# Second attention of a two-block kernel: the sink becomes a 257th logit column, fillers are split in halves, output chunk 0 is finished first

## The chip, the cores and the metric

The kernel runs on one core of one Trainium2 chip. The metric is the device time of one execution in microseconds (us), lower is better. Three runs of the kernel before gave 1569.63, 1569.12 and 1566.43 us (median 1569.12). Traces are taken in an execution of their own.

## What is computed

Two transformer blocks over 512 tokens of width 1024 in fp32. The first block has two layers: a gated linear recurrence with a convolutional feed-forward part, and then a sliding-window attention with a sink, again with a feed-forward part. The second block mixes pooling, a forgetting attention and a memory attention. The change lies in the sliding-window attention, which has 16 query heads of width 64, 4 key/value heads and a window of 128 over 128-token blocks:

```python
logits = einsum(q, kk) * scale + bias            # 128 queries x 256 keys (block j-1 and j)
logits = where(mask, logits, -inf)
m = maximum(logits.max(-1), sink)                # sink: one learned number per query head
p = exp(logits - m[..., None])
denom = p.sum(-1) + exp(sink - m)
o = einsum(p, vv) / denom
return o.reshape(B, S, D) @ w_out
```

## The kernel before

Everything is written by hand, engine by engine, in program order, with semaphores between the engines. Each large matrix product is done in three fp32r matmuls (high*high, low*high, high*low parts), so activations and weights are kept as a high and a low half: `AH`/`AL`, `OH`/`OL`, `WH`/`WL`. Weights come in 1 MB chunks, in one order, through two slots: SyncE loads `RAW`, ScalarE writes the high half (`split_hi`, `split_next`, L1155), GpSimd writes the low half in four instructions (`split_cols` L444, `split_rows` L453), TensorE uses the chunk and releases its slot (`w_used`). `EXTRAS` are a few chunks with slots of their own, whose low half VectorE writes (`extra_low`, L1767).

The second attention (calls `sw_...`) works in 16 units, `SW_UNITS`: a unit is one pair of heads b (two heads, x) with two query blocks (t), so four rows of 256 logits. For unit i:

- TensorE `sw_score(i)` (L868) makes the scores in `bank[0]`. It waits for the logits of unit i-1, and for every fourth unit for the next query chunk `QB`.
- VectorE `sw_logits(i)`: scale and bias into `PL` (L2001), maximum of the row (L2004), minimum with the negated sink (L2006), sink minus maximum (L2008), which releases the unit (`l_ready`).
- ScalarE `sw_expo(i)`: the exponential of the sink (L1447), then of the four rows with their sums (L1450).
- VectorE `sw_weights(i)`: sum plus sink (L2013), reciprocal (L2015), four row scalings (L2018), which release `p_ready`.
- TensorE `sw_turn(i)` (L881), eight transposes of `PL`; ScalarE copies them to `PT` (L1472); TensorE `sw_weigh(i)` (L895) multiplies by the values `VT`; for every second unit VectorE `sw_finish` writes `OH`/`OL` (L2025, L2027).

The order of the engines: VectorE does logits(i+1), perhaps finish, weights(i). ScalarE does expo(i+1), the copy of unit i, and after units 1, 5 and 9 `sw_query`: it copies the next query chunk (L1456) and splits one more weight chunk (L1155), whose low half GpSimd then makes. TensorE does, for u from 0 to 15, score(u+2), turn(u), weigh(u-1), and fills with independent work, called fillers here: quarters of the query chunks 1 to 3 (`sw_piece`, 12 matmuls of 512 columns) for u up to 9, and pieces of the first two output chunks N_SO and N_SO+1 (`sw_mixed(j, ms)`, output blocks `ms` of chunk j, 6 matmuls each) from u=10. What is left of these follows the last unit, and then `last_rows` uses N_SO+2 and N_SO+3, which are split only when the slots of N_SO and N_SO+1 are released.

Of the kernel before, what the change touches and what calls it, by code (L numbers as in the profile page):

```python
# [29 lines left out]
P = 128  # L30
# [59 lines left out]
def build(nc, stream, x_t, mem_t, params, consts, masks, sinks, rel_in, w_pool, out):  # L90
# [6 lines left out]
    with ExitStack() as ctx:  # L97
# [25 lines left out]
        SMALL = sb("SMALL", [P, 4, 3, 4])  # L123
# [5 lines left out]
        INV = sb("INV", [P, 2, T])  # L129
        par = {k: PAR[:, a:b] for k, (a, b) in PCOL.items()}  # L130
# [3 lines left out]
        NMAX, SUMS, SNK, RDEN = (SMALL[:, i] for i in range(4))  # L134
# [12 lines left out]
        with ExitStack() as s:  # L147
# [11 lines left out]
            with ExitStack() as s1:  # L159
                BIAS = sb("BIAS", [P, SWH, 2 * P], F32, s1)  # L160
                KT = sb("KT", [P, 2, T], F32, s1)
                VT = sb("VT", [P, TT, 2 * P], F32, s1)
                QB = sb("QB", [P, 8, T], F32, s1)
                PL = sb("PL", [P, 3, 4, 2 * P], F32, s1)
                PT = sb("PT", [P, 2, 8, P], F32, s1)
# [67 lines left out]
        def bk(i):  # L233
            return bank[i // 2][:, i % 2]
# [41 lines left out]
        sg_made, pool_w_loaded = sem("sg_made"), sem("pool_w_loaded")  # L276
# [200 lines left out]
        def _(pe):  # L477
# [362 lines left out]

            def sw_piece(c, piece):

                if piece == 0 and c == 1:
                    pe.wait_ge(v_copied_sw, 1)
                if piece == 0 and c > 1:
                    pe.wait_ge(qb_copied, c)
                n = SQ_CHUNK[c]
                col_chunk(n, slot(n), (bk(6), bk(7)), AH, AL, ks=(2 * piece, 2 * piece + 1))
# [59 lines left out]
            for u in range(16):  # L908
                if u + 2 < 16:
                    sw_score(u + 2)  # L910
                if u == 0:
                    pe.wait_ge(qb_copied, 1)
                sw_turn(u)
                if u == 0:
                    sw_piece(1, 1)
                    sw_piece(1, 2)
                if u == 1:
                    sw_piece(1, 3)
                    pe.wait_ge(v_copied_sw, 1)
                if u == 5:  # L920
                    sw_piece(2, 3)
                if u == 9:
                    sw_piece(3, 3)
                if u == 15:
                    pe.wait_ge(l_ready, 16)
                    sw_mixed(0, (2, 3))
                if u:
                    sw_weigh(u - 1)
                if 2 <= u < 5:
                    sw_piece(2, u - 2)  # L930
                if 6 <= u < 9:
                    sw_piece(3, u - 6)
                if u == 10:
                    pe.wait_ge(qb_copied, 4)
                    pe.wait_ge(o_ready, 10)
                    sw_mixed(0, (0,))
                if u == 11:
                    sw_mixed(0, (1,))
                if u == 12:
                    pe.wait_ge(o_ready, 12)  # L940
                    sw_mixed(1, (0,))
                if u == 13:
                    sw_mixed(1, (1,))
            sw_weigh(15)
            pe.wait_ge(pt_ready, 16)
            sw_mixed(0, (4, 5))
            sw_mixed(1, (2, 3))
            pe.wait_ge(o_ready, 16)
            sw_mixed(0, (6, 7))
            sw_mixed(1, (4, 5, 6, 7))  # L950
# [197 lines left out]
        def _(act):  # L1148
# [312 lines left out]
            sw_query(0)  # L1461
            sw_expo(0)
# [3 lines left out]
            for i in range(16):  # L1466
# [118 lines left out]
        def _(dve):  # L1585
# [397 lines left out]
            SINK3 = SINK[:, :].rearrange("p (o x b) -> p o x b", o=2, x=2)  # L1983
            BIAS5 = BIAS[:, :, :].rearrange("p (o x b) s -> p o x b s", o=2, x=2)

            def sw_logits(i):
# [3 lines left out]
                nmax, snk = (a[:, s].rearrange("p (x t) -> p x t", t=2) for a in (NMAX, SNK))  # L1990
                bias = BIAS5[:, b // 4, :, b % 4]
                sink = SINK3[:, b // 4, :, b % 4].unsqueeze(2).broadcast_to([P, 2, 2])
# [6 lines left out]
                for t in range(2):  # L1999
                    lo = P if tiles[t] == 0 else 0  # L2000
                    dve.scalar_tensor_tensor(rows[:, :, t, lo:], bank[0][:, :, 256 * t + lo:256 * t + 256], SCALE, bias[:, :, lo:],  # L2001
                                             ALU.mult, ALU.add)
                dve.drain()
                dve.tensor_reduce(nmax, rows, AX_X, ALU.max, negate=True)  # L2004
                dve.drain()
                dve.scalar_tensor_tensor(nmax, sink, -1.0, nmax, ALU.mult, ALU.min)  # L2006
                dve.drain()
                dve.tensor_tensor(snk, sink, nmax, ALU.add).then_inc(l_ready, 1)  # L2008

            def sw_weights(i):  # L2010
                s = i % 3
                dve.wait_ge(p_exp, i + 1)
                dve.tensor_tensor(SUMS[:, s], SUMS[:, s], SNK[:, s], ALU.add)  # L2013
                dve.drain()
                dve.reciprocal(RDEN[:, s], SUMS[:, s])  # L2015
                dve.drain()
                for r in range(4):
                    ins = dve.tensor_scalar(PL[:, s, r], PL[:, s, r], RDEN[:, s, r:r + 1], None, ALU.mult)  # L2018
# [316 lines left out]
```

## Time and profile before

| | |
|---|---|
| median of three runs | 1569.12 us (1566.43 to 1569.63) |
| the profiled execution | 1567.07 us, span 1565.3 us |
| TensorE busy (PE) | 1497.5 us, 96% |
| VectorE busy (DVE) | 900.5 us, 58% |
| ScalarE busy (ACT) | 611.4 us, 39% |
| GpSimd busy (POOL) | 510.7 us, 33% |
| mean granted TensorE clock | 0.992 |

The time is that of the whole program; the span runs from its first to its last recorded instruction. PE is the matmul row of the profile, DVE, ACT and POOL the rows of VectorE, ScalarE and GpSimd. The second attention's units lie between 737 and 855 us of the span, and the end of its output product between 855 and 887 us.

### The profile page before, as it was taken

To read this page: it belongs to the slowest core of one execution; us is meant where nothing else is said; L and a number is where in the kernel's file an instruction comes from. 1 tells how busy PE (TensorE), PEld (TensorE's weight loads), DVE (VectorE), ACT (ScalarE), POOL (GpSimd) and SP (SyncE) were. 2 spreads that over 40 slices of the span, in tenths; PEclk is the share of its full clock that TensorE was granted. 3 is DMA by queue.
4 is the path that set the end of the run, shared out by engine and by line. 5 is a ranking of instruction groups with operands and counts; after the bars stand their busy time and mean duration, and the time that the engine had idled before them with its cause. 6 is when DMAs were issued, how large, how long until landed. Compare 5 with 4: busy or idle time off the path is not lost.

```text
span 1565.3 us, 21457 instructions
## 1 busy us (share of the span) xinstructions
PE 1497.5 (96%) x8174; PEld 1254.0 (80%) x8174; DVE 900.5 (58%) x1315; ACT 611.4 (39%) x768; POOL 510.7 (33%) x380
## 2 busy tenths in 40 slices
PE   7999999999999999999997999999999989999889
PEld 5888888798888888889775888888888887777667
DVE  7778686576566550145686576556620283655741
ACT  3554455344322231235564442332221254555520
POOL 3000002215454554532210335545444533323212
PEclk9999999999999999999999999999999999999999
DMA  8511111412322223332202112232222222312201
GB/s 226 131 55 55 69 67 54 148 68 81 108 82 106 88 99 108 107 108 82 81 28 81 54 53 89 102 107 80 107 88 100 103 98 83 108 58 74 88 27 54
DMA packets 22583, 137.22 MB, mean 88 GB/s; under 512 B 2488, under 2 KB 4840, under 8 KB 7280
## 3 DMA queue, kind: packets, MB, share of 16 engines
q1 hardware_dynamic: 17280, 124.79, 22.5%
q10 hardware_dynamic: 5232, 11.45, 3.0%
q8 instruction: 48, 0.79, 0.2%
q14 instruction: 23, 0.19, 0.0%
HBM read 132.02 MB, written 4.21 MB: 87 GB/s over the span
## 4 chain that ended last, share of the span: by engine, by line
issue 58%; POOL 25%; PE 14%; ACT 1%; DVE 1%; ACTq 0%; DMA 0%; DVEq 0%; POOLq 0%; SPq 0%
POOL WL L444 16%; POOL WL L453 9%; PE pair L480 4%; PE pair L481 3%; PE pair L482 3%; PE pair L1048 1%; PE pair L1035 1%; ACT WH L1155 1%; PE pair L967 1%; ACTq L1486 0%; DVE PL L2146 0%; DMA RAW<-stream 0%; PE pair L1025 0%; ACT PL L1490 0%; ACT L1509 0%
## 5 line engine op out<-in xcount | busy, mean ns | idle before, releaser
L444 POOL TENSOR_TENSOR WL<-RAW,WH 128x512 fp32r<-128x512 f32 x240 | 327.5, 1397 | 490.7 <-ACT WH L1155 490.7
L480 PE MATMUL pair<-AH,WH 128*128 128x512 f32 (+1 forms) x1240 | 472.6, 381 | 14.3 <-POOL WL L444 11.4
L481 PE MATMUL pair<-AL,WH 128*128 128x512 f32 (+1 forms) x1240 | 463.0, 373 | 0.0
L482 PE MATMUL pair<-AH,WL 128*128 128x512 f32 (+1 forms) x1240 | 462.7, 373 | 0.0
L1155 ACT ACTIVATE WH<-RAW 128x2048 fp32r<-128x2048 f32 x108 | 206.6, 1914 | 474.9 <-PE pair L482 460.4
L453 POOL TENSOR_TENSOR WL<-RAW,WH 128x512 fp32r<-128x512 f32 x136 | 183.0, 1377 | 545.2 <-ACT WH L1155 545.2
L480 PEld LDWEIGHTS pair<-AH,WH 128*128 128x128 f32 x1240 | 233.6, 188 | 60.1 <-POOL WL L444 11.4
L482 PEld LDWEIGHTS pair<-AH,WL 128*128 128x128 f32 x1240 | 233.4, 188 | 41.8
L481 PEld LDWEIGHTS pair<-AL,WH 128*128 128x128 f32 x1240 | 233.7, 188 | 40.5 <-issue 1.9
L1940 DVE TENSOR_SCALAR CA<-pair,PAR 128x512 f32<-128x512 f32 x88 | 67.3, 806 | 148.2 <-PE pair L482 145.2
L480 PE MATMUL pair<-GH,WH 128*128 (+2 forms) x416 | 150.4, 361 | 0.0
L482 PE MATMUL pair<-GH,WL 128*128 (+2 forms) x416 | 149.9, 360 | 0.0
L481 PE MATMUL pair<-GL,WH 128*128 (+2 forms) x416 | 149.9, 360 | 0.0
L1945 DVE SCALAR_TENSOR_TENSOR CA<-pair,PAR,CA 128x510 f32<-128x510 f32 (+1 forms) x176 | 123.8, 745 | 14.4 <-issue 13.8
L480 PE MATMUL pair<-OH,WH 128*128 128x512 f32 (+1 forms) x256 | 90.3, 353 | 2.4 <-POOL WL L453 2.4
L480 PEld LDWEIGHTS pair<-GH,WH 128*128 128x128 f32 x416 | 78.2, 188 | 13.5 <-POOL WL L453 0.2
L481 PEld LDWEIGHTS pair<-GL,WH 128*128 128x128 f32 x416 | 78.2, 188 | 13.3
L482 PEld LDWEIGHTS pair<-GH,WL 128*128 128x128 f32 x416 | 78.2, 188 | 13.0
L481 PE MATMUL pair<-OL,WH 128*128 128x512 f32 (+1 forms) x256 | 87.6, 342 | 0.0
L482 PE MATMUL pair<-OH,WL 128*128 128x512 f32 (+1 forms) x256 | 87.4, 341 | 0.0
L1767 DVE TENSOR_TENSOR WL<-RAW,WH 128x1024 fp32r<-128x1024 f32 x14 | 20.1, 1481 | 103.6 <-ACT WH L1169 103.5
L480 PE MATMUL pair<-WH,AH 128*128 128x256 f32 (+1 forms) x192 | 59.9, 312 | 3.8 <-DVE AL L1851 2.9
(245 smaller groups left out, 2012.9 us busy)
## 6 DMA issues: line engine op xcount, KB each, us to landing
RAW<-stream SPq DMA_DIRECT2D x115, 1024.0 KB, 4.8
H<-x_t SPq DMA_DIRECT2D x3, 1024.0 KB, 8.9
bias_rows<-ROWS ACTq DMA_DIRECT2D x1, 2048.0 KB, 24.9
BIAS<-bias_rows ACTq DMA_DIRECT2D x1, 2048.0 KB, 7.7
FBC<-forget_rows ACTq DMA_DIRECT2D x4, 512.0 KB, 4.0
out<-H ACTq DMA_DIRECT2D x8, 256.0 KB, 2.0
H<-x_t SPq DMA_DIRECT2D x2, 512.0 KB, 6.1
CON<-consts ACTq DMA_DIRECT2D x1, 513.5 KB, 4.3
```

The costliest lines, as they stand in the source:

```text
L444: pool.tensor_tensor(WL[w][:, part], RAW[raw][:, part], WH[w][:, part].bitcast(F32), ALU.subtract).then_inc(w_lo, 1)
L453: pool.tensor_tensor(wl[:, :, part], raw[:, :, part], wh[:, :, part].bitcast(F32), ALU.subtract).then_inc(w_lo, 1)
L480: pe.matmul(out_, wh, xh, start=start, stop=False, skip_group_check=shared)
L481: pe.matmul(out_, wh, xl, start=False, stop=False, skip_group_check=shared)
L482: return pe.matmul(out_, wl, xh, start=False, stop=stop, skip_group_check=shared)
L967: pe.matmul(bk(5), con["mean64"], SQH[:, :], start=True, stop=True).then_inc(n_summed, 1)
L1035: mm = pe.transpose(bk(2 + x)[:, at:at + P], PL2[:, i % 3, x, at:at + P], con["ident"])
L1048: mm = pe.matmul(bk(4)[64 * x:64 * x + 64, n * P:n * P + P], (VM if kind == "mem" else VF)[:, kb, c0:c0 + 64], PT2[:, i % 2, x, 256 * t + ...
L1155: act.activation(WH[w][:, :], RAW[raw][:, :], ACT.Copy).then_inc(w_hi, 1)
L1767: dve.tensor_tensor(WL[w][:, part], RAW[w][:, part], WH[w][:, part].bitcast(F32), ALU.subtract).then_inc(e_lo, 1)
L1940: dve.tensor_scalar(out_[:, c], src[:, c], tap[2], CONVB[:, layer, ab, blk], ALU.mult, ALU.add)
L1945: ins = dve.scalar_tensor_tensor(out_[:, c, d:T], src[:, c, 0:T - d], CONVW[:, layer, 2 - d, ab, blk], out_[:, c, d:T], ALU.mult, ALU.add)
```

## The change

1. `PL` rows are 264 wide instead of 256. ScalarE copies the sink of the head into column 256 (`sw_sink`): three times ahead of unit 0, and after the copy of unit i for unit i+3. The maximum runs over 257 columns and the exponentials with their sums too. L2006, L2008 and L2013 on VectorE and L1447 on ScalarE are gone, and `SMALL` loses a row. The maximum waits for the sink's copy (`sink_put`).
2. The fillers of TensorE: for u=1, 5, 9 the quarter of a query chunk stands ahead of turn(u) instead of behind it; for u=3, 4, 7, 8 half of it (`sw_half`, 6 matmuls) stands ahead of turn(u) and half behind weigh(u-1); the output pieces of u=10 to 13 stand at u=11 to 14, ahead of turn(u), and that of u=15 too.
3. Behind the last unit, output blocks 6 and 7 of chunk 0 come ahead of blocks 2 and 3 of chunk 1.

```diff
-        SMALL = sb("SMALL", [P, 4, 3, 4])
+        SMALL = sb("SMALL", [P, 3, 3, 4])
...
-                PL = sb("PL", [P, 3, 4, 2 * P], F32, s1)
+                PL = sb("PL", [P, 3, 4, 2 * P + 8], F32, s1)
...
+            def sw_half(c, piece, m):
+                if (piece, m) == (0, 0):
+                    pe.wait_ge(qb_copied, c)
+                n = SQ_CHUNK[c]
+                wh, wl = wcols(slot(n))
+                for k in (2 * piece, 2 * piece + 1):
+                    if m == 0 and k % 2 == 0:
+                        lo_ready(n, k // 2)
+                    mm = three(bk(6 + m), wh[:, k, m * P:m * P + P], wl[:, k, m * P:m * P + P], AH[:, k], AL[:, k], k == 0, k == KB - 1)
+                if (piece, m) == (3, 1):
+                    mm.then_inc(w_used, 1)
...
+                if u == 1:
+                    sw_piece(1, 3)
+                if u in (3, 4, 7, 8):
+                    sw_half(2 + u // 6, (u - 1) % 4 - 1, 0)
+                if u in (5, 9):
+                    sw_half(2 + u // 6, 3, 0)
+                    sw_half(2 + u // 6, 3, 1)
+                if u == 11:
+                    sw_mixed(0, (0,))
+                if u == 12:
+                    sw_mixed(0, (1,))
+                if u == 13:
+                    pe.wait_ge(o_ready, 12)
+                    sw_mixed(1, (0,))
+                if u == 14:
+                    sw_mixed(1, (1,))
+                if u == 15:
+                    pe.wait_ge(l_ready, 16)
+                    sw_mixed(0, (2, 3))
                 sw_turn(u)
                 if u == 0:
                     sw_piece(1, 1)
                     sw_piece(1, 2)
                 if u == 1:
-                    sw_piece(1, 3)
                     pe.wait_ge(v_copied_sw, 1)
-                if u == 5:
-                    sw_piece(2, 3)
-                if u == 9:
-                    sw_piece(3, 3)
-                if u == 15:
-                    pe.wait_ge(l_ready, 16)
-                    sw_mixed(0, (2, 3))
                 if u:
                     sw_weigh(u - 1)
-                if 2 <= u < 5:
-                    sw_piece(2, u - 2)
-                if 6 <= u < 9:
-                    sw_piece(3, u - 6)
+                if u in (2, 6):
+                    sw_half(2 + u // 6, 0, 0)
+                    sw_half(2 + u // 6, 0, 1)
+                if u in (3, 4, 7, 8):
+                    sw_half(2 + u // 6, (u - 1) % 4 - 1, 1)
                 if u == 10:
                     pe.wait_ge(qb_copied, 4)
                     pe.wait_ge(o_ready, 10)
-                    sw_mixed(0, (0,))
-                if u == 11:
-                    sw_mixed(0, (1,))
-                if u == 12:
-                    pe.wait_ge(o_ready, 12)
-                    sw_mixed(1, (0,))
-                if u == 13:
-                    sw_mixed(1, (1,))
+            pe.wait_ge(pt_ready, 16)
             sw_weigh(15)
-            pe.wait_ge(pt_ready, 16)
             sw_mixed(0, (4, 5))
-            sw_mixed(1, (2, 3))
             pe.wait_ge(o_ready, 16)
             sw_mixed(0, (6, 7))
-            sw_mixed(1, (4, 5, 6, 7))
+            sw_mixed(1, (2, 3, 4, 5, 6, 7))
             last_rows(2, 3, OH, OL)
...
-                act.activation(SNK[:, s], SNK[:, s], ACT.Exp)
                 for r in range(4):
-                    row = PL[:, s, r]
+                    row = PL[:, s, r, 0:2 * P + 1]
...
+            def sw_sink(i):
+                _, b, _ = SW_UNITS[i]
+                act.activation(PL[:, i % 3, :, 2 * P].rearrange("p (x t) -> p x t", t=2),
+                               SINK3[:, b // 4, :, b % 4].unsqueeze(2).broadcast_to([P, 2, 2]), ACT.Copy).then_inc(sink_put, 1)
...
+            for i in range(3):
+                sw_sink(i)
             sw_expo(0)
...
                 act.activation(PT[:, i % 2].rearrange("p (x k) c -> p x (k c)", x=2), bank[1][:, :, :], ACT.Copy).then_inc(pt_ready, 1)
+                if i + 3 < 16:
+                    sw_sink(i + 3)
...
-                dve.tensor_reduce(nmax, rows, AX_X, ALU.max, negate=True)
-                dve.drain()
-                dve.scalar_tensor_tensor(nmax, sink, -1.0, nmax, ALU.mult, ALU.min)
-                dve.drain()
-                dve.tensor_tensor(snk, sink, nmax, ALU.add).then_inc(l_ready, 1)
+                dve.wait_ge(sink_put, i + 1)
+                dve.tensor_reduce(nmax, rows[:, :, :, 0:2 * P + 1], AX_X, ALU.max, negate=True).then_inc(l_ready, 1)
...
-                dve.tensor_tensor(SUMS[:, s], SUMS[:, s], SNK[:, s], ALU.add)
-                dve.drain()
```

On VectorE, the logits and weights of one unit. Before (from logits(9) to the start of logits(10)):

```order
L2001 SCALAR_TENSOR_TENSOR PL<-pair,BIAS 128x2x256 x2
L2004 TENSOR_REDUCE SMALL<-PL 128x4
L2006 SCALAR_TENSOR_TENSOR SMALL<-SINK,SMALL 128x4
L2008 TENSOR_TENSOR SMALL<-SINK,SMALL 128x4
L2013 TENSOR_TENSOR SMALL<-SMALL 128x4
L2015 RECIPROCAL SMALL<-SMALL 128x4
L2018 TENSOR_SCALAR PL<-PL,SMALL 128x256 x4
L1997 MEMSET PL 128x2x128
```

The same place now:

```order
L2021 SCALAR_TENSOR_TENSOR PL<-pair,BIAS 128x2x256 x2
L2025 TENSOR_REDUCE SMALL<-PL 128x4
L2030 RECIPROCAL SMALL<-SMALL 128x4
L2033 TENSOR_SCALAR PL<-PL,SMALL 128x256 x4
L2017 MEMSET PL 128x2x128
```

Three small instructions of a unit are gone; the rest keeps its order.

On TensorE, u=11: score(13), turn(11), weigh(10) and a piece of the output product (`OH`, `OL` with `WH`, `WL`). Before:

```order
L868 MATMUL pair<-KT,QB 128x256 x4
L881 MATMUL pair<-CON,PL 128x128 x8
L895 MATMUL pair<-PT,VT 64x128 x6
L480 MATMUL pair<-OH,WH 128x512
L481 MATMUL pair<-OL,WH 128x512
L482 MATMUL pair<-OH,WL 128x512
```

Now:

```order
L879 MATMUL pair<-KT,QB 128x256 x4
L481 MATMUL pair<-OH,WH 128x512
L482 MATMUL pair<-OL,WH 128x512
L483 MATMUL pair<-OH,WL 128x512
L481 MATMUL pair<-OH,WH 128x512
L482 MATMUL pair<-OL,WH 128x512
L483 MATMUL pair<-OH,WL 128x512
L892 MATMUL pair<-CON,PL 128x128 x8
L906 MATMUL pair<-PT,VT 64x128 x6
```

The six matmuls that stood behind weigh now stand between the scores and the transposes.

On ScalarE, what follows expo(6): the copy of unit 5, the query chunk, the split. Before:

```order
L1472 ACTIVATE PT<-pair 128x1024
L1456 ACTIVATE QB<-pair 128x1024
L1155 ACTIVATE WH<-RAW 128x2048
L1447 ACTIVATE SMALL<-SMALL 128x4
L1450 ACTIVATE PL,SMALL<-PL,SMALL 128x256 x4
```

Now:

```order
L1492 ACTIVATE PT<-pair 128x1024
L1468 ACTIVATE PL<-SINK 128x4
L1474 ACTIVATE QB<-pair 128x1024
L1169 ACTIVATE WH<-RAW 128x2048
L1463 ACTIVATE PL,SMALL<-PL,SMALL 128x257 x4
```

The small instruction ahead of the exponentials is gone, and one of the same size stands behind the copy of the transposes, ahead of the query copy. (Lines shift by the added code.)

## Rows read from the trace of the kernel before

**Rows 1.** Waits of TensorE, 753 to 890 us: total, times, longest.
```profile
PE pair L881 <- DVE PL L2018: 10.9, 6, 3.1
PE pair L480 <- POOL WL L453: 2.1, 1, 2.1
PE pair L868 <- DVE SMALL L2008: 1.0, 1, 1.0
```

**Rows 2.** Timeline of TensorE, units 2 to 6: start, duration, instructions, [idle before].
```profile
766.21 0.93 PE L868 MATMUL pair<-KT,QB 64*128 64x128 f32 x8 [0.27 <-ACT QB L1456]
...
768.09 1.15 PE L895 MATMUL pair<-PT,VT 128*64 128x128 f32 x16
...
772.10 1.14 PE L868 MATMUL pair<-KT,QB 64*128 64x256 f32 x8
774.96 1.09 PE L881 MATMUL pair<-CON,PL 128*128 128x128 f32 x8 [1.72 <-DVE PL L2018]
...
791.77 0.49 PE L868 MATMUL pair<-KT,QB 64*128 64x128 f32 x4 [0.27 <-ACT QB L1456]
```

**Rows 3.** Timeline of TensorE, the last units.
```profile
832.94 1.15 PE L895 MATMUL pair<-PT,VT 128*64 128x128 f32 x16
835.61 1.14 PE L868 MATMUL pair<-KT,QB 64*128 64x256 f32 x8
...
847.99 1.97 PE L881 MATMUL pair<-CON,PL 128*128 128x128 f32 x8 [3.09 <-DVE PL L2018]
853.34 1.80 PE L895 MATMUL pair<-PT,VT 128*64 128x128 f32 x28
```

**Rows 4.** Timeline of VectorE: logits(11), weights(10), then logits(12).
```profile
813.90 1.22 DVE L2004 TENSOR_REDUCE SMALL<-PL 128x4 f32<-128x1024 f32 x1
815.20 0.16 DVE L2006 SCALAR_TENSOR_TENSOR SMALL<-SINK,SMALL 128x4 f32<-128x4 f32 x1
815.43 0.16 DVE L2008 TENSOR_TENSOR SMALL<-SINK,SMALL 128x4 f32<-128x4 f32 x1
815.51 0.16 DVE L2013 TENSOR_TENSOR SMALL<-SMALL 128x4 f32<-128x4 f32 x1
815.74 0.18 DVE L2015 RECIPROCAL SMALL<-SMALL 128x4 f32<-128x4 f32 x1
816.00 1.14 DVE L2018 TENSOR_SCALAR PL<-PL,SMALL 128x256 f32<-128x256 f32 x4
...
819.38 1.22 DVE L2004 TENSOR_REDUCE SMALL<-PL 128x4 f32<-128x1024 f32 x1
820.67 1.00 DVE L2006 SCALAR_TENSOR_TENSOR SMALL<-SINK,SMALL 128x4 f32<-128x4 f32 x1
821.75 1.15 DVE L2008 TENSOR_TENSOR SMALL<-SINK,SMALL 128x4 f32<-128x4 f32 x1
```

**Rows 5.** Timeline of ScalarE and of GpSimd at the query chunk of unit 9.
```profile
816.23 1.03 ACT L1456 ACTIVATE QB<-pair 128x1024 f32<-128x1024 f32 x1 [1.72 <-PE pair L482]
817.15 1.90 ACT L1155 ACTIVATE WH<-RAW 128x2048 fp32r<-128x2048 f32 x1
...
819.13 4.98 POOL L453 TENSOR_TENSOR WL<-RAW,WH 128x512 fp32r<-128x512 f32 x4 [20.52 <-ACT WH L1155]
```

**Rows 6.** Timeline of VectorE and of GpSimd in the memory attention, from 1372 us.
```profile
1375.04 3.01 DVE L2146 TENSOR_SCALAR PL<-PL,SMALL 128x256 f32<-128x256 f32 x4 [0.44 <-issue]
...
1372.31 5.07 POOL L444 TENSOR_TENSOR WL<-RAW,WH 128x512 fp32r<-128x512 f32 x4 [12.81 <-ACT WH L1155]
```

**Rows 7.** Windows: length, busy and count of PE, PEld, DVE, ACT, POOL, then PEclk.
```profile
827.40:830.60 3.20, 3.20 (x15) 2.48 (x13) 2.47 (x9) 2.16 (x7) 0.00 (x0) 0.50 0.30 125
847.90:851.10 3.20, 3.12 (x12) 2.83 (x13) 0.03 (x1) 1.11 (x2) 0.00 (x0) 0.50 0.00 0
```

**Rows 8.** Timeline of GpSimd and ScalarE at the end of the output product.
```profile
865.76 11.97 POOL L453 TENSOR_TENSOR WL<-RAW,WH 128x512 fp32r<-128x512 f32 x8 [41.65 <-ACT WH L1155]
...
869.37 1.92 ACT L1155 ACTIVATE WH<-RAW 128x2048 fp32r<-128x2048 f32 x1 [1.88 <-PE pair L482]
```

More of the change, by code:

```diff
@@ L129, in build @@
         INV = sb("INV", [P, 2, T])
+        SINK3 = SINK[:, :].rearrange("p (o x b) -> p o x b", o=2, x=2)
         par = {k: PAR[:, a:b] for k, (a, b) in PCOL.items()}
@@ L133, in build @@
         CONVB = par["conv_b"].rearrange("p (l a j) -> p l a j", l=2, a=2)
-        NMAX, SUMS, SNK, RDEN = (SMALL[:, i] for i in range(4))
+        NMAX, SUMS, RDEN = (SMALL[:, i] for i in range(3))
         with ExitStack() as s:
@@ L275, in build @@
         fox_v_mm, fox_v, vm_copied, half_mm, o_taken = (sem(n) for n in ("fox_v_mm", "fox_v", "vm_copied", "half_mm", "o_taken"))
-        sg_made, pool_w_loaded = sem("sg_made"), sem("pool_w_loaded")
+        sg_made, pool_w_loaded, sink_put = sem("sg_made"), sem("pool_w_loaded"), sem("sink_put")
         z_abs, z_exp, f_made, f_stored = (sem(n) for n in ("z_abs", "z_exp", "f_made", "f_stored"))
@@ L844, in sw_piece @@
                     pe.wait_ge(v_copied_sw, 1)
-                if piece == 0 and c > 1:
-                    pe.wait_ge(qb_copied, c)
                 n = SQ_CHUNK[c]
@@ L1981, in _ @@
             layer_norm(1)
-            SINK3 = SINK[:, :].rearrange("p (o x b) -> p o x b", o=2, x=2)
             BIAS5 = BIAS[:, :, :].rearrange("p (o x b) s -> p o x b s", o=2, x=2)
@@ L1989, in sw_logits @@
                 rows = PL[:, s].rearrange("p (x t) s -> p x t s", t=2)
-                nmax, snk = (a[:, s].rearrange("p (x t) -> p x t", t=2) for a in (NMAX, SNK))
+                nmax = NMAX[:, s].rearrange("p (x t) -> p x t", t=2)
                 bias = BIAS5[:, b // 4, :, b % 4]
-                sink = SINK3[:, b // 4, :, b % 4].unsqueeze(2).broadcast_to([P, 2, 2])
                 dve.drain()
@@ L2000, in sw_logits @@
                     lo = P if tiles[t] == 0 else 0
-                    dve.scalar_tensor_tensor(rows[:, :, t, lo:], bank[0][:, :, 256 * t + lo:256 * t + 256], SCALE, bias[:, :, lo:],
+                    dve.scalar_tensor_tensor(rows[:, :, t, lo:2 * P], bank[0][:, :, 256 * t + lo:256 * t + 256], SCALE, bias[:, :, lo:],
                                              ALU.mult, ALU.add)
                 dve.drain()
-                dve.tensor_reduce(nmax, rows, AX_X, ALU.max, negate=True)
-                dve.drain()
-                dve.scalar_tensor_tensor(nmax, sink, -1.0, nmax, ALU.mult, ALU.min)
-                dve.drain()
-                dve.tensor_tensor(snk, sink, nmax, ALU.add).then_inc(l_ready, 1)
+                dve.wait_ge(sink_put, i + 1)
+                dve.tensor_reduce(nmax, rows[:, :, :, 0:2 * P + 1], AX_X, ALU.max, negate=True).then_inc(l_ready, 1)
             def sw_weights(i):
@@ L2017, in sw_weights @@
                 for r in range(4):
-                    ins = dve.tensor_scalar(PL[:, s, r], PL[:, s, r], RDEN[:, s, r:r + 1], None, ALU.mult)
+                    ins = dve.tensor_scalar(PL[:, s, r, 0:2 * P], PL[:, s, r, 0:2 * P], RDEN[:, s, r:r + 1], None, ALU.mult)
                 ins.then_inc(p_ready, 1)
```

## The prediction, made before the changed kernel ran

> **What bounds the kernel now.** I read the waits of TensorE first, because TensorE is busy for 96% of the span and is the only engine whose idle time can be won. In and behind the second attention it waits 10.9 us in six places for the row scalings of VectorE, 1.0 us for VectorE's logits, and 2.1 us for a low half of GpSimd at the output product [rows 1]. Then I read the timelines of the engines. TensorE shows two regimes. With 12-matmul fillers four units take 25.56 us (766.21 to 791.77) and TensorE idles only 0.27 + 1.72 of them [rows 2]: it is the bound. In the last five units the fillers are 6 matmuls, and it waits at nearly every turn, 3.09 us at the last one [rows 3]: there VectorE is the bound, whose logits, finish and weights stand in one line. Last I read the granted clock: it falls to 0.50, which is 1.2 GHz, for 3.2 us each at 827.4 and 847.9, both times just behind idle stretches of TensorE [rows 7].
>
> **How I cost it.** The change alters orders on three engines that release each other, so I carried it forward step by step: each step starts when its engine is free and its last releaser is done, plus the 0.05 us or so that rows show between engines, with durations from the rows. On the order of before this gives scores(8) at 791.69 and scores(12) at 817.16 (trace: 791.77 [rows 2], and 817.31, just behind the query copy that ends at 817.26 [rows 5]) and the last transposes at 847.07 (847.99 [rows 3]; the clock fall at 827 is the difference). So it may be trusted to some tenths of a us. With the new order it gives the terms below.
>
> **VectorE's unit.** From the end of the maximum (813.90 + 1.22 = 815.12) to the logits' release (815.59) two small instructions cost 0.47 us; L2013 delays the reciprocal by 0.23 more [rows 4]. The memory attention of this kernel has exactly the new sequence, and there the reciprocal follows the maximum at once. So weights end 0.70 us earlier in each unit. One more column in the maximum and in an exponential costs about a nanosecond a row: nothing. The small exponential's 0.11 us in front of ScalarE's rows goes too, and the sink's copy, of the same size, stands behind the copy of the transposes. The new wait for it costs nothing: that copy is issued three units ahead, about 5 us before the maximum needs it. The scalings still read 256 columns in one run, so I leave their 1.14 us for four [rows 4]; were the wider row pitch to make them slower, only five units are on the path. The bounds of the 0.70 are 0.47 (nothing won at L2013) and 0.70.
>
> The Trainium skill, page "VectorE: DVE Perf Modes", section on the TRN2 errata, gives 58 + N cycles for an SBUF source, an estimate of 0.065 us for each of the three. By that the unit would win 0.2 us and not 0.70, and the stage some 2.5 us less. The rows decide, since they show the gaps too.
>
> **GpSimd beside VectorE.** At unit 12 the two removed instructions took 1.00 and 1.15 us in place of 0.16 [rows 4], while GpSimd's four splits ran from 819.13 to 824.11 [rows 5]; the same at units 4 and 8. That is 1.84 us gone each time. But the scalings then come 2.5 us earlier, into the same GpSimd stretch, and the memory attention shows what four scalings cost there: 3.01 us instead of 1.14, each waiting for the end of one GpSimd instruction [rows 6]. In the steps this makes weights(3), (7) and (11) end 1.55 us later than alone. For units 3 and 7 that is hidden behind the half filler with 0.8 us to spare; for unit 11 it is not.
>
> This is a rule of the Trainium skill that speaks against the change: page "SBUF — State Buffer", section "Who interferes with whom", says that a scaling in the two-port mode and a GpSimd instruction exclude each other for the whole instruction. The trace agrees, with the 3.01 us. By the rule each scaling issued under GpSimd waits separately, which is the sum here; without it the forecast would be 1.5 us better.
>
> **Units 0 to 11 (query fillers).** Splitting a filler costs: 12 matmuls take 772.10 - 768.09 - 1.07 = 2.94 us [rows 2], six take 835.61 - 832.94 - 1.08 = 1.59 [rows 3]. Four splits cost 4 x 0.26 = 1.0 us. At u=1, 5, 9 the filler now stands ahead of the transposes, so scores(4), (8), (12) come right behind weigh, while the query copy comes behind the copy of the transposes: 1.09 transposes + 1.02 copy + 0.12 sink + 1.03 query copy, against 1.02 + 0.86 or 1.08 of TensorE work. It waits 1.40 us where it waited 0.27 [rows 2, 5], three times: +3.4. What goes are the 1.72 us waits at turn(3) and turn(7) [rows 2]: -3.4. So scores(12) start at 818.42 instead of 817.31: **+1.1 us**. The first eleven units win nothing.
>
> **Units 11 to 15 (VectorE bound).** From scores(12) to the last transposes before takes 847.99 - 817.31 = 30.7 us. Here four logits save 0.47 and five weights 0.23 (-3.0), the GpSimd collisions change by -1.84 + 1.55, and the clock fall at 827 with its 0.75 us on the path is absent; against that some scores come 0.5 us later, behind a filler and a turn. The steps give 845.51 - 818.42 = 27.1: **-3.6 us**.
>
> **Behind the last transposes.** Before, 847.99 to 855.07 (the end of the weighing) is 7.1 us, with a 12-matmul filler of 2.94 in it and the clock at half for 3.2 us, which costs 1.56 [rows 3, 7]. Now that filler lies ahead of the transposes, in the 3.09 us of waiting. Left are transposes, the two weighings and a 0.33 wait for the last copy, 3.3 us: **-3.8 us**.
>
> **Output product.** 20 pieces of work stay. Chunk 0 is used up 12 matmuls earlier, 2.8 to 2.9 us. That releases ScalarE's split and GpSimd's four instructions for N_SO+2 by as much, and the wait of 2.1 us [rows 1] goes. N_SO+3 becomes next: its slot is released at 869.37 as before, its fourth low part would be there at 869.37 + 1.92 + 5.0 = 876.4, and TensorE asks for it at 876.45 [rows 8]. That is just hidden, bounds 0 to 0.5: **-2.1 us**.
>
> **Sum.** 1.1 - 3.6 - 3.8 - 2.1 = -8.4 us. It counts on no clock fall. One like that at 827 costs 0.75 to 1.6; between 821 and 829 the new order still idles 0.4 + 1.8 + 0.9 us, where the old one idled 3.0 and fell. I take off 0.4 for it: **-8.0 us**. The profiled execution took 1567.07 us, so its like would take 1559.1; it lies 2.05 below the median of the three runs, 1569.12, and on the median the forecast is 1561.1 us. Everything behind the stage moves as a block, since its loads are released by the progress of the engines.
>
> **Rivals.**
> - *Half of it* (chance 0.20): the collisions are worse than 1.55 in units 3 and 7, where only 0.8 us of cover is left, and the clock falls as often as before. Both falls back cost 2.3, two more collisions up to 1.5 each beyond the cover, giving 2.5 to 5 us, 1564 to 1566.5. For it speaks that idle stretches of 1.4 us come in at three new places; against it that the 1.72 us idle of before brought no fall.
> - *No change that can be told* (0.08): the change does not do what it says, because the row scalings move wholly under GpSimd at each query chunk and scores wait for the query copy by more than 1.4 us, say 3 us when the split stands ahead. That makes units 0 to 11 lose 5 us more. Then 1566 to 1571.
> - *More* (0.08): VectorE's shorter unit lets TensorE close nearly all of the 14.0 us of waits [rows 1] and the slow clock. The 1.40 waits stand against it: 10 to 12 us, 1557 to 1559.
> - *Slower* (0.05): the clock. From 818 to 829 TensorE idles in four short pieces. If it were granted half speed there and did not come back until the end of the units at 849, 31 us at half would cost up to 15 us, 1566 to 1576. It ends above before if half speed lasts over 16 us. The two falls of before lasted 3.2 us each and ended in dense work [rows 7], which comes back at 849 at the latest.
> - The forecast, 5 to 10 us won, has 0.59.
>
> **How the numbers follow.** About 0.2% (3.1 us) is what a measurement of this kernel can tell from no change. Faster by more: the forecast, the rival with more, and most of the half (0.15): 0.82. Within: the rest of the half and the third case: 0.13. Slower: 0.05. The range goes from 1557, which takes in the case with more, to 1566, which takes in most of the half; outside are about two in ten.
>
> **What would show it.** The waits of TensorE for the scalings should fall from 10.9 to under 3 us, with turn(3), turn(7) and the last turn gone; scores(4), (8), (12) should wait about 1.4 us each for the query copy; four scalings of weights(3), (7), (11) should take 2.5 to 3 us; the 2.1 us wait at N_SO+2 should be gone, with none or a short one at N_SO+3; the clock windows should show at most one fall. The prediction is wrong if a new wait stands on `sink_put`, if the clock falls at scores(4) or (8), or if the stretch ahead of scores(12) grows by more than 2 us.

## The result and the profile after

The changed kernel takes 1557.14 us (median of 4 runs, 1556.08 to 1557.67) beside 1567.84 for the kernel before (4 runs, 1566.43 to 1569.63). The ratio is 0.9921, 95% interval 0.9907 to 0.9934, which is 10 to 15 us; the medians themselves differ by 10.7 us, a ratio of 0.9932, and the two profiled executions by 9.8 (1567.07 and 1557.29). The forecast of 8.0 us had the sign and the mechanisms, and was too small.

The page's heading and its busy times (busy us, share, instructions) for the kernel after:

```profile
span 1555.5 us, 21361 instructions
PE 1494.0 (96%) x8174; PEld 1250.0 (80%) x8174; DVE 889.1 (57%) x1267; ACT 610.7 (39%) x768; POOL 510.5 (33%) x380
```

VectorE has 48 instructions less, three for each unit, and 11.4 us less work. TensorE runs the same number of matmuls, but it is not only its idle time that went. Over the stage (from a mark at its start to the layer norm behind it, both defined in the next section) its row reads, first before and then after (length, busy and count of PE, PEld, DVE, ACT, POOL, then PEclk):

```profile
749.86:888.46 138.60, 122.62 (x837) 96.73 (x837) 92.64 (x202) 68.90 (x167) 32.02 (x24) 0.98 0.17 62
750.39:879.00 128.61, 119.63 (x836) 94.46 (x836) 83.48 (x157) 68.39 (x165) 32.24 (x24) 1.00 0.19 66
```

So 7.0 of the 10.0 us were idle time, and 3.0 us were busy time: the same matmuls, some of them at the lower clock in the kernel before. The waits of TensorE after, 753 to 890 us (total, times, longest), to be read against [rows 1]:

```profile
PE pair L879 <- ACT QB L1474: 3.8, 3, 1.3
PE pair L892 <- DVE PL L2033: 2.1, 3, 1.4
PE pair L583 <- DVE H L1810: 1.5, 1, 1.5
PE pair L879 <- DVE SMALL L2025: 1.2, 2, 0.8
PE pair L906 <- ACT PT L1492: 0.3, 1, 0.3
```

The waits for the row scalings fell from 10.9 to 2.1 us, that for GpSimd at the output product is gone, and three waits of 1.3 us for the query copy are new in size: they were 0.27 us each. The timeline of TensorE after shows the four units of [rows 2], and then the end of [rows 3]. The matmuls of the fillers (L481 to L483) between these rows are left out:

```profile
767.79 0.93 PE L879 MATMUL pair<-KT,QB 64*128 64x128 f32 x8 [1.26 <-ACT QB L1474]
768.65 1.09 PE L892 MATMUL pair<-CON,PL 128*128 128x128 f32 x8
769.67 1.15 PE L906 MATMUL pair<-PT,VT 128*64 128x128 f32 x16
773.69 1.13 PE L879 MATMUL pair<-KT,QB 64*128 64x256 f32 x8
776.25 1.04 PE L892 MATMUL pair<-CON,PL 128*128 128x128 f32 x8
777.22 0.93 PE L906 MATMUL pair<-PT,VT 128*64 128x128 f32 x12
779.68 0.93 PE L879 MATMUL pair<-KT,QB 64*128 64x128 f32 x8
...
785.65 1.14 PE L879 MATMUL pair<-KT,QB 64*128 64x256 f32 x8
789.58 1.04 PE L892 MATMUL pair<-CON,PL 128*128 128x128 f32 x8
790.55 0.93 PE L906 MATMUL pair<-PT,VT 128*64 128x128 f32 x12
792.74 0.93 PE L879 MATMUL pair<-KT,QB 64*128 64x128 f32 x8 [1.26 <-ACT QB L1474]
...
844.39 1.09 PE L892 MATMUL pair<-CON,PL 128*128 128x128 f32 x8
845.41 0.93 PE L906 MATMUL pair<-PT,VT 128*64 128x128 f32 x12
846.68 1.12 PE L906 MATMUL pair<-PT,VT 128*64 128x128 f32 x16 [0.35 <-ACT PT L1492]
```

From the first marked scores to the second, four units take 24.95 us where they took 25.56. Within them TensorE waits once, the 1.26 us at their start. turn(3) at 776.25 does not wait although its scalings run into GpSimd until 775.35 (their row is the first below), since the half filler stands in front of it. At the end the last transposes wait for nothing, where they waited 3.09 us. The timelines of VectorE and of GpSimd after, at units 11 and 12 (the counterpart of [rows 4, 5]):

```profile
772.79 2.56 DVE L2033 TENSOR_SCALAR PL<-PL,SMALL 128x256 f32<-128x256 f32 x4
...
819.72 1.22 DVE L2025 TENSOR_REDUCE SMALL<-PL 128x4 f32<-128x1028 f32 x1
821.03 0.69 DVE L2040 CAST OH<-pair 128x512 fp32r<-128x512 f32 x1
821.80 0.69 DVE L2042 TENSOR_TENSOR OL<-pair,OH 128x512 fp32r<-128x512 f32 x1
822.41 0.17 DVE L2030 RECIPROCAL SMALL<-SMALL 128x4 f32<-128x4 f32 x1
822.65 2.53 DVE L2033 TENSOR_SCALAR PL<-PL,SMALL 128x256 f32<-128x256 f32 x4
825.35 1.29 DVE L2021 SCALAR_TENSOR_TENSOR PL<-pair,BIAS 128x512 f32<-128x512 f32 x2 [0.16 <-issue]
826.71 1.22 DVE L2025 TENSOR_REDUCE SMALL<-PL 128x4 f32<-128x1028 f32 x1
827.85 0.17 DVE L2030 RECIPROCAL SMALL<-SMALL 128x4 f32<-128x4 f32 x1
828.10 1.14 DVE L2033 TENSOR_SCALAR PL<-PL,SMALL 128x256 f32<-128x256 f32 x4
```

```profile
819.47 5.04 POOL L454 TENSOR_TENSOR WL<-RAW,WH 128x512 fp32r<-128x512 f32 x4 [19.85 <-ACT WH L1169]
```

The maximum over 1028 elements still takes 1.22 us, and the four scalings of unit 11 take 2.53 us while GpSimd works and 1.14 us in unit 12, when it does not. The granted clock after, in windows, shows no fall where [rows 7] showed two:

```profile
820.00:836.00 16.00, 13.16 (x104) 9.62 (x101) 14.24 (x28) 11.05 (x37) 4.51 (x4) 1.00 0.19 66
836.00:852.00 16.00, 15.14 (x112) 11.78 (x111) 9.42 (x19) 6.96 (x12) 0.00 (x0) 1.00 0.38 132
```

### The profile page after: what moved, and what is told of

Read it like the earlier page. It is cut to its first block, busy times and chain, and to the rows that moved or that the text cites. A ratio compares the mean times of both kernels' runs of the same rounds, so it can differ in the third digit from the quotient of the medians.

```text
span 1555.5 us, 21361 instructions
## 1 busy us (share of the span) xinstructions
PE 1494.0 (96%) x8174; PEld 1250.0 (80%) x8174; DVE 889.1 (57%) x1267; ACT 610.7 (39%) x768; POOL 510.5 (33%) x380
## 4 chain that ended last, share of the span: by engine, by line
issue 58%; POOL 25%; PE 14%; ACT 1%; DVE 1%; ACTq 0%; DMA 0%; DVEq 0%; POOLq 0%; SPq 0%
POOL WL L445 16%; POOL WL L454 9%; PE pair L481 4%; PE pair L482 3%; PE pair L483 3%; PE pair L1062 1%; PE pair L1049 1%; ACT WH L1169 1%; PE pair L981 1%; ACTq L1508 0%; DVE PL L2161 0%; DMA RAW<-stream 0%; PE pair L1039 0%; ACT PL L1512 0%; ACT L1531 0%
## 5 line engine op out<-in xcount | busy, mean ns | idle before, releaser
L481 PE MATMUL pair<-AH,WH 128*128 128x512 f32 (+1 forms) x1240 | 473.6, 382 | 14.6 <-POOL WL L445 11.5
L483 PE MATMUL pair<-AH,WL 128*128 128x512 f32 (+1 forms) x1240 | 462.9, 373 | 0.0
L481 PEld LDWEIGHTS pair<-AH,WH 128*128 128x128 f32 x1240 | 233.6, 188 | 62.1 <-POOL WL L445 11.8
L483 PEld LDWEIGHTS pair<-AH,WL 128*128 128x128 f32 x1240 | 233.4, 188 | 42.2
L481 PE MATMUL pair<-GH,WH 128*128 (+2 forms) x416 | 149.6, 360 | 0.1
L483 PE MATMUL pair<-GH,WL 128*128 (+2 forms) x416 | 149.0, 358 | 0.0
L481 PE MATMUL pair<-OH,WH 128*128 128x512 f32 (+1 forms) x256 | 89.2, 349 | 0.4 <-POOL WL L454 0.4
L481 PEld LDWEIGHTS pair<-GH,WH 128*128 128x128 f32 x416 | 78.0, 188 | 14.0 <-POOL WL L454 0.5
L483 PEld LDWEIGHTS pair<-GH,WL 128*128 128x128 f32 x416 | 77.9, 187 | 13.3
L483 PE MATMUL pair<-OH,WL 128*128 128x512 f32 (+1 forms) x256 | 86.6, 338 | 0.0
L1251 ACT ACTIVATE DD<-DD 128x1024 f32<-128x1024 f32 x28 | 29.5, 1055 | 86.7 <-DVE DD L1672 86.7
```

The source lines that it names most:

```text
L481: pe.matmul(out_, wh, xh, start=start, stop=False, skip_group_check=shared)
L483: return pe.matmul(out_, wl, xh, start=False, stop=stop, skip_group_check=shared)
L1251: act.activation(DD[:, lv % 2], DD[:, lv % 2], ACT.Exp).then_inc(level_exp, 1)
```

## The stage against landmarks

The stretch ahead of the stage differs by up to 3 us between executions of any kernel here (the mark below falls between 748.85 and 752.01 us), so I compare the stage against a mark inside it: the start of the filler that waits 1.11 us for the values' copy `VT` ahead of scores(2), on TensorE. The landmarks are the start of scores(12), of the last transposes, the end of the last weighing, and the start of the first sum of the layer norm behind the output product. Each number is the landmark's time less the mark's time, both read from the timeline of TensorE:

```
kernel                        mark   scores(12)  turn(15)  units end  first norm sum   against before
before                       749.86     67.45      98.13     105.21      138.60              -
after                        750.39     67.26      94.00      97.34      128.61             -9.99
after, second trace          751.60     67.28      94.02      97.36      128.63             -9.97
sink column only             752.01     65.19      91.53      98.65      131.72             -6.88
fillers only                 751.27     67.74      97.75     101.04      135.95             -2.65
chunk 0 first only           749.98     67.42      98.11     105.22      136.56             -2.04
after, halves not split      751.33     68.28      95.01      98.35      129.69             -8.91
after, short GpSimd splits   748.85     67.25      92.59      95.93      127.20            -11.40
query copy first             751.15     63.28      90.46      93.80      125.08            -13.52
query copy first, again      750.16     63.28      90.47      93.80      125.08            -13.52
the same, late split         749.05     63.28      88.67      92.00      123.35            -15.25
```

Two traces of one kernel agree within 0.02 us here, while the whole times spread over 2 to 7 us. Nothing of the change is lost ahead of the mark: from the start of GpSimd's low halves ahead of the mark to the mark itself is 11.98 us before (737.88 to 749.86) and 11.97 us after (738.42 to 750.39).

The spread comes with the granted clock. Runs of the kernel before that took 1566.64 and 1567.01 us had a mean clock of 0.992, those of 1571.8 and 1571.77 us had 0.989. The second trace of the changed kernel has the clock at 0.50 between about 1281 and 1287 us, where the first has 1.00, and its execution took 2.1 us longer. So the causes are read from this table, and the whole times say that they arrive at the end. In nine of the ten comparisons the medians differ from before by 0.5 to 2.6 us more than the table (the first runs of the query copy differ by 0.5 less); what that rest is was not settled.

## The experiments

**Each part alone.** Parts 1, 2 and 3 of the change were put into the kernel before, one at a time.

Sink column only (all of part 1; TensorE's order and the end as before). Its main lines are:

```diff
-                act.activation(SNK[:, s], SNK[:, s], ACT.Exp)
...
+                act.activation(PL[:, i % 3, :, 2 * P].rearrange("p (x t) -> p x t", t=2),
+                               SINK3[:, b // 4, :, b % 4].unsqueeze(2).broadcast_to([P, 2, 2]), ACT.Copy).then_inc(sink_put, 1)
...
-                dve.scalar_tensor_tensor(nmax, sink, -1.0, nmax, ALU.mult, ALU.min)
...
-                dve.tensor_tensor(snk, sink, nmax, ALU.add).then_inc(l_ready, 1)
...
-                dve.tensor_tensor(SUMS[:, s], SUMS[:, s], SNK[:, s], ALU.add)
```

> Only part 1: the sink as a column put by ScalarE, three VectorE instructions of a unit gone; the order of TensorE is that of before. Theory A (each part wins by its own waits; the steps of the prediction): the units end 5.2 us earlier, since weights come 0.7 us earlier in each unit and the two collisions with GpSimd at units 4, 8, 12 go; TensorE still waits about 2.9 us at the last transposes and the 2.1 us wait at the output product stays. In time -5 us, up to -7 if a fall of the clock goes with it. Rival B (the gain is that of the clock, which stops falling when TensorE idles less): turns still wait 2.1 and 2.9 us in the last units, so the clock still falls there and little more than 2 us is won. Rival C (TensorE's order makes the gain): under 2 us.

Measured: 1561.36 us (5 runs) beside 1569.21 (21 runs), ratio 0.9955 (0.9941 to 0.9969); 6.9 us by the landmarks. TensorE's waits, 753 to 890 us:

```profile
PE pair L882 <- DVE PL L2020: 7.0, 6, 2.9
PE pair L481 <- POOL WL L454: 2.1, 1, 2.1
PE pair L869 <- ACT QB L1461: 0.8, 3, 0.3
```

Its timeline at the last units:

```profile
843.54 1.43 PE L882 MATMUL pair<-CON,PL 128*128 128x128 f32 x8 [2.85 <-DVE PL L2020]
848.93 1.80 PE L896 MATMUL pair<-PT,VT 128*64 128x128 f32 x28
```

The units end 6.6 us earlier (5.2 were expected, without a change of the clock). The clock no longer falls at 827 and still falls behind the 2.85 us wait (0.72 on the mean of 842 to 848). Theory A holds: the waits at turn(3) and turn(7) are 0.60 instead of 1.72, and that alone brings scores(12) 2.26 us forward. Rival C falls, since this part makes two thirds of the gain with TensorE's order in place. Rival B can explain a part and not the whole: over the stage (752.01 to 883.73 us) TensorE is busy for 120.45 us, 2.2 less than before, which is the most that the clock can have given, and idle for 11.3 us, 4.7 less than before.

Fillers only (all of part 2, in TensorE's loop; the first filler is shown and the others are moved as in the change):

```diff
                 if u == 1:
+                    sw_piece(1, 3)
...
                 sw_turn(u)
...
                 if u == 1:
-                    sw_piece(1, 3)
```

> Only part 2: the fillers between scores and transposes, VectorE and ScalarE as before, the end of the output product as before. Theory A as put on record (six matmuls 1.60 us, twelve 2.94 wherever they stand) gives -1.2 us for the units; with what the trace of the changed kernel shows (six matmuls ahead of transposes 1.50, twelve 2.86) -2.1 us. The waits at scores(4), (8), (12) rise to 1.3 us, those at turn(3), turn(7) fall to 0.2. A fall of the clock behind the last transposes would go, since the wait of 3.1 us there goes: another -1.6. So -1 to -4 us. Rival B (clock): -3 to -4 us with no fall left in the windows. Rival C (order makes the gain): -6 us or more.

Measured: 1565.64 us (11 runs) beside 1569.21, ratio 0.9977 (0.9968 to 0.9986). The units end 4.2 us earlier, and 1.5 of these are lost again in the output product. These are the waits of TensorE:

```profile
PE pair L878 <- DVE SMALL L2022: 4.5, 3, 2.7
PE pair L878 <- ACT QB L1470: 3.5, 3, 1.2
PE pair L480 <- POOL WL L453: 2.1, 1, 2.1
PE pair L891 <- DVE PL L2032: 1.8, 3, 1.2
```

The window behind its 2.1 us wait for GpSimd shows the clock:

```profile
871.30:874.50 3.20, 3.20 (x18) 3.20 (x17) 0.00 (x0) 0.00 (x0) 3.20 (x3) 0.53 0.79 317
```

The waits move from the turns to the scores: VectorE's line is as long as before, so the time is waited for elsewhere. Both clock falls of before are gone and one has come at a place that had none, behind a wait that before was as long (2.06 us) and had no fall behind it. The longest wait of this kernel, 2.69 us ahead of scores(13), had none behind it either. So the order of fillers by itself is worth 2.65 us here, inside the 1 to 4 us of theory A: over the stage (751.27 to 887.22 us) TensorE idles 2.3 us less than before and is busy 0.4 us less. The 1.5 us that are lost with the new fall were in no forecast.

Chunk 0 first only (part 3):

```diff
+            pe.wait_ge(pt_ready, 16)
             sw_weigh(15)
-            pe.wait_ge(pt_ready, 16)
             sw_mixed(0, (4, 5))
-            sw_mixed(1, (2, 3))
             pe.wait_ge(o_ready, 16)
             sw_mixed(0, (6, 7))
-            sw_mixed(1, (4, 5, 6, 7))
+            sw_mixed(1, (2, 3, 4, 5, 6, 7))
```

The moved wait changes nothing, since `sw_weigh(15)` waits for the same copy itself.

> Only part 3: chunk 0's last blocks ahead of chunk 1's. Theory A: the wait of 2.06 us for GpSimd at the third output chunk goes and nothing takes its place: -2.1 us. Rival: the fourth chunk's low half becomes late, a wait up to 1 us at its second pair of blocks: -1 us.

Measured: 1565.92 us (11 runs) beside 1569.21, ratio 0.9981 (0.9971 to 0.9990); 2.04 us by the landmarks, and the wait for GpSimd is gone from the list with nothing in its place. The feared wait for the fourth chunk did not come.

The three alone sum to 11.6 us, the change is 10.0. Parts 1 and 2 each shorten the same waits at turn(3) and turn(7) and each remove the clock fall at 827, and that can be won only once. This explains the sign of the difference; its size was not added up, and the fall that only the fillers alone have works against it.

**The halves ahead of the transposes.** The changed kernel with both halves behind weigh at u=3, 4, 7, 8:

```diff
-                if u in (3, 4, 7, 8):
-                    sw_half(2 + u // 6, (u - 1) % 4 - 1, 0)
...
                 if u in (3, 4, 7, 8):
+                    sw_half(2 + u // 6, (u - 1) % 4 - 1, 0)
                     sw_half(2 + u // 6, (u - 1) % 4 - 1, 1)
```

> The changed kernel, but at u=3, 4, 7, 8 both halves stand behind weigh, none ahead of the transposes. Question: was the split the loss that the prediction made of it (4 x 0.26 us) and does the half ahead of turn(3), turn(7) hide the collision of the scalings? Theory A: without the halves ahead turn(3) and turn(7) wait 0.8 us each for the scalings that GpSimd delays, 1.6 in all; the saved joins give back 0.5 (as the changed kernel's trace has them) or 1.0 (as on record): the kernel is 0.5 to 1.2 us slower than the changed one, so 9 to 10 us faster than before. Rival (splitting costs what was forecast, hiding is worth less): as fast or up to 0.5 us faster than the changed one, waits at turn(3), turn(7) under 0.3.

Measured: 1558.79 us (5 runs) beside 1569.21, ratio 0.9937 (0.9923 to 0.9950); by the landmarks 1.08 us slower than the changed kernel. turn(3) and turn(7) wait 0.59 and 0.58 us. The other half says what a split costs: from scores(4) to scores(8) this kernel takes 25.44 us with 1.26 and 0.59 of waiting, which leaves 23.59 of work; the changed one takes 24.95 with 1.26, which leaves 23.69. Counted so, two splits cost 0.10 us, 0.05 each. That is a lower bound: the 0.59 us are counted from the recorded end of the scores, and without a wait transposes start 0.07 us ahead of that end (786.81, against 785.74 + 1.14, in the kernel before). With it a split costs 0.09 us, still not 0.26.

**The collision with GpSimd.** The changed kernel, with GpSimd's low halves of six weight chunks cut to 16 of 512 columns in each instruction (the rest of these low halves is left out of the computation). The main lines are:

```diff
-                    part = slice(512 * q, 512 * q + 512)
+                    part = slice(512 * q, 512 * q + width[0])
...
+            width[0] = 16
             span(split_cols, N_KV + 2, 4)
-            span(split_rows, N_SO, 4)
+            span(split_rows, N_SO, 2)
+            width[0] = 512
+            span(split_rows, N_SO + 2, 2)
```

> The changed kernel, but GpSimd's low halves of six weight chunks (four of keys, values and queries, two of the output product) cover 16 columns instead of 512 in each instruction, so the rest of those low halves is left out. Theory A (the port collision delays the scalings of units 3, 7, 11 by 1.4 us and only that of unit 11 is on the path): four scalings take 1.14 us everywhere, turn(11) waits under 0.3 instead of 1.43, the units end 1.3 to 1.6 us earlier than in the changed kernel. Rival (the collision is hidden everywhere by other waits): no difference, the wait moves to scores(13) or scores(14).

Measured: 1554.49 us (5 runs) beside 1568.02 (9 runs), ratio 0.9914 (0.9901 to 0.9928); 1.41 us under the changed kernel by the landmarks. Below are the scalings of unit 11 on VectorE, the low halves on GpSimd, and TensorE's wait for the scalings in 753 to 890 us:

```profile
821.10 1.14 DVE L2038 TENSOR_SCALAR PL<-PL,SMALL 128x256 f32<-128x256 f32 x4
```

```profile
817.92 0.75 POOL L456 TENSOR_TENSOR WL<-RAW,WH 128x16 fp32r<-128x16 f32 x4 [24.17 <-ACT WH L1174]
```

```profile
PE pair L897 <- DVE PL L2038: 0.7, 2, 0.5
```

The scalings are back at 1.14 us, and the wait of 1.43 us at turn(11) is gone. scores(12) stand at 67.25 as in the changed kernel (67.26), so the collisions of units 3 and 7 cost nothing there: the half fillers hide them. By the rule of the Trainium skill, page "SBUF — State Buffer", section "Who interferes with whom", a scaling in the two-port mode and a GpSimd instruction exclude each other for the whole instruction, and the traces agree, with 2.53 us against 1.14 for the four scalings of unit 11.

**The waits for the query copy.** The changed kernel with ScalarE's query copy of units 1, 5 and 9 ahead of its copy of the transposes:

```diff
+                if i in (1, 5, 9):
+                    sw_copy((i + 3) // 4)
                 act.wait_ge(p_turned, i + 1)
...
                 if i in (1, 5, 9):
-                    sw_query((i + 3) // 4)
+                    split_next(SQ_CHUNK[(i + 3) // 4])
```

> The changed kernel, but ScalarE copies the query chunk (units 1, 5, 9) ahead of the copy of the transposes; the weight split stays behind it. Theory A (the waits of 1.26 us at scores(4), (8), (12) are the one new cost of the fillers' order, and they are on the path): the three waits go, nothing takes their place but 0.1 us; the units end 3.7 us earlier than in the changed kernel, 14 us under before. Rival (VectorE's line or the collision with GpSimd is the true bound there, so the time comes back at turn(7) and turn(11)): under 1.5 us won, with waits of 2.5 us or more at turn(11).

> The kernel with the query copy first again, for a comparison in the same call: 13 to 14 us under before, 3.5 us less than the changed kernel at the landmarks of the trace, with 1.9 us of waiting at turn(11).

Measured: 1554.95 us (5 runs) beside 1568.02, ratio 0.9917 (0.9903 to 0.9930), and again 1553.28 (5 runs) beside 1569.39 (9 runs), ratio 0.9895 (0.9875 to 0.9915). By the landmarks it is 3.53 us under the changed kernel, twice. Below are the waits of TensorE, 753 to 890 us, and the scalings of unit 11:

```profile
PE pair L892 <- DVE PL L2038: 2.6, 3, 1.9
PE pair L879 <- DVE SMALL L2030: 1.2, 2, 0.8
```

```profile
819.43 2.99 DVE L2038 TENSOR_SCALAR PL<-PL,SMALL 128x256 f32<-128x256 f32 x4
```

The three waits of 1.26 us (3.8 in all) are gone, and part of them comes back at turn(11), which waits 1.89 instead of 1.43: more of the scalings now meet GpSimd (2.99 us for four).

**Both.** The same kernel, with ScalarE's split of the second output chunk after unit 11 instead of unit 9, so that GpSimd works between two sets of scalings:

```diff
-                if i in (1, 5, 9):
+                if i in (1, 5, 11):
                     split_next(SQ_CHUNK[(i + 3) // 4])
```

> The kernel with the query copy first, and ScalarE's split of the second output chunk behind the copy of unit 11 instead of unit 9, so that GpSimd's four instructions fall between the scalings of units 12 and 13 and not on those of unit 11. Theory A (the wait of 1.9 us at turn(11) is the port collision and nothing else): the four scalings of unit 11 take 1.14 us instead of about 3, turn(11) waits under 0.5, units 12 and 13 keep 1.14 to 1.4, the chunk is there for its first use at u=13: 1.4 to 1.8 us faster than the same kernel with the early split, some 15 us under before. Rival: the collision moves on to unit 12 or 13, or the later load makes the output product wait: under 0.5 us.

Measured: 1552.17 us (4 runs) beside 1569.39, ratio 0.9892 (0.9876 to 0.9908). VectorE's scalings of units 11 to 13 and GpSimd:

```profile
817.34 1.14 DVE L2038 TENSOR_SCALAR PL<-PL,SMALL 128x256 f32<-128x256 f32 x4
821.38 1.14 DVE L2038 TENSOR_SCALAR PL<-PL,SMALL 128x256 f32<-128x256 f32 x4
827.39 1.20 DVE L2038 TENSOR_SCALAR PL<-PL,SMALL 128x256 f32<-128x256 f32 x4
```

```profile
822.66 5.00 POOL L454 TENSOR_TENSOR WL<-RAW,WH 128x512 fp32r<-128x512 f32 x4 [26.57 <-ACT WH L1169]
```

turn(11) no longer waits, and the stage is 1.73 us shorter than with the early split (1.80 us at the units' end, 92.00 and 93.80). The whole times cannot tell these two versions apart (medians 1.1 us apart, intervals overlapping); the landmarks can. It beats both kernels: 15.25 us under before at the landmark, 5.3 under the changed one.

**The changed kernel again.**

> The changed kernel again, as it is, beside the others of this call: 10 us under before. Its landmarks in the trace should stand within 0.1 us of the first trace against the start of the units, with no fall of the clock. If the difference to before comes out at 8 or at 12 us, the part of the forecast's miss that is not in the stage's waits is a matter of the runs and not of the kernel.

Measured: 1557.59 us (5 runs) beside 1568.02, ratio 0.9931 (0.9918 to 0.9945), and landmarks within 0.02 us of the first trace. So the stage accounts for 10.0 us. The first ratio shows more (0.0079 of 1567.84 is 12.4 us at its middle), and this one 10.8 us (8.6 to 12.9); both intervals hold 10.7, and what lies above 10.0 is not found in the stage.

## Why the prediction was two to three us short

The mechanisms came as forecast; what failed is the size of two terms in the step for units 0 to 11. The terms below are compared with the landmarks of the stage.

- **VectorE's unit** (0.70 us earlier in each): right. From the start of the maximum to the start of the scalings took 2.10 us (813.90 to 816.00) and takes 1.39 (826.71 to 828.10). The reciprocal starts 0.08 us before the recorded end of the maximum (827.85 against 826.71 + 1.22 in the trace after). The wait for the sink's copy never ended an idle time: the copy starts 3.2 us or more ahead of the maximum (766.63 against 769.86 is among the shortest), where the forecast said about 5. The wider rows cost nothing: four scalings take 1.14 us.
- **GpSimd beside VectorE**: right. The 1.84 us are gone and 1.4 us are back (forecast 1.55), hidden in units 3 and 7, on the path in unit 11. The experiment with short splits shows the last two.
- **Units 0 to 11**: this is the step that failed. "So scores(12) start at 818.42 instead of 817.31: +1.1 us" was measured as 67.26 - 67.45 = -0.2 us, 1.3 us off. Two terms of it were mis-sized. The first is the splits, "4 x 0.26 = 1.0 us". (Its own figures give 2 x 1.59 - 2.94 = 0.24 each.) They cost 0.05 to 0.11 us each: a half in front of transposes takes 776.25 - 774.75 = 1.50 us and not 1.59, the half in front of scores 779.68 - 778.08 = 1.60, and the transposes behind a filler 0.97 to the next instruction and not 1.02. With 2.94 for the whole filler that is 0.11. I had taken the price of a filler from places where other instructions stood behind it. Over these units the splits and the three moved quarters cost 0.3 us in all (-0.2, less 3 x 0.99 of longer query waits, plus 2 x 1.72 of waits at the turns), where the forecast counted the same way has 1.2. The second is the query wait, which is 1.26 us and not 1.40, three times: 0.4 us in all. The sum for it used recorded durations, and the copy of the transposes with its 1.02 us leads to the next instruction in 0.92 (765.71 to 766.63).
- **Units 11 to 15**: forecast -3.6, measured 94.00 - 67.26 - (98.13 - 67.45) = -3.9. Of the 0.3 us between them about 0.15 is the collision at unit 11 (1.39 us more for the scalings and not 1.55); the joins of the four fillers ahead of transposes may be the rest, which is not shown.
- **Behind the last transposes**: forecast -3.8, measured 3.34 - 7.08 = -3.7. Right, with the hidden filler and the absent clock fall.
- **Output product**: forecast -2.1, measured 31.27 - 33.39 = -2.1. Right, and the part alone gives 2.04.
- **The clock**: "I take off 0.4 for it" was not needed, since there was no fall in the stage.

Together these are 1.3 + 0.3 + 0.4 us, and 10.0 in place of 8.0. The whole times add 0.7 us to that (10.7), which no term of the stage explains. The rivals "half of it" and "no change" fall with the landmarks. The rival with "more" has the size, since the result lies at the lower end of its 10 to 12 us, but not its reason: the query waits stay, and 9.0 us of idle time are left in the stage. The waits that the prediction called the price of the new order were real, and removing them is worth what it said, 3.5 us.

## What to carry to other kernels

Removing a few tiny instructions from the middle of a chain that sets the pace is worth their gaps and not only their length (0.70 us a unit for three instructions of 0.16), and more where another engine makes them wait (1.00 and 1.15 us in place of 0.16); but look at what slides into the same stretch instead. Independent work that hides a wait is best put in front of the waiting instruction, and then the next wait is on whatever was queued behind it (here a copy that could simply go first). When whole times spread over several us, compare traces from a mark inside the stage: here two traces of one kernel agreed within 0.02 us.

## What the runs showed of the hardware that was not expected

- TensorE's transposes start 0.17 us before the recorded end of a 512-column matmul in front of them (776.25, against 776.02 + 0.40 in the kernel after), scores only 0.07 us before it (773.69, against 773.37 + 0.39). The recorded ends are the profile's model, but the starts say the same: from the last matmul of the filler to transposes is 0.23 us, to scores 0.32. A price for a block of matmuls depends on what follows it.
- In this stage the granted clock fell to 0.50, for some 3 us each time, in before (two falls, one behind 1.02 and 1.96 us close together and one behind 3.09 us), in chunk 0 first alone (the same two), in the sink column alone (one, behind 2.85 us of idle time) and in the fillers alone (one, behind a wait of 2.06 us that left the clock alone in before and in the sink column alone). It did not fall behind single waits of 1.92 us (sink column alone) and 2.69 us (fillers alone), nor in the changed kernel, with single waits up to 1.4 us, nor in the versions with the query copy first, with one of 1.89 us. Which idle stretch brings a fall is not settled by these runs, and the length of a single wait does not decide it.
- Two executions of one kernel can differ in the falls. In both traces of the changed kernel TensorE waits 2.77 us for `AL` in the later part (the wait ends at 1280.00 in the first and at 1281.18 in the second). The first stays at 1.00 over the ten us behind it; the second is at 0.50 from 1281 to 1287.
